# Fourteen of 24 groups of modulation vectors: from TensorE in four stages to VectorE inside the first MLP

## What is computed

```python
silu_c, silu_cc = silu(c), silu(c_ctx)                   # two vectors of 1024
for i in range(2):
    mod_x = silu_c @ w_mod[i] + b_mod[i]                  # 6 x 1024 values
    mod_c = silu_cc @ w_mod[i] + b_mod[i]
    # shift, scale, gate of the mixer; shift, scale, gate of the MLP
    hx = rmsnorm(x) * (1 + sc_x) + sh_x                   # the same for ctx
    yx = conv_module(hx) if i == 0 else attention(hx, hc)
    x = x + g_x * rmsnorm(yx)                             # ctx too in layer 0
    fx = rmsnorm(x) * (1 + scf_x) + shf_x
    x = x + gf_x * rmsnorm((silu(fx @ w1) * (fx @ w3)) @ w2)
```

## Time and profile before

| | |
|---|---|
| median of 3 runs | 1949.99 us (1949.28 to 1951.88) |
| the profiled execution's own time | 1947.4 us |
| its span in the profile | 1945.6 us |
| mean granted TensorE clock | 0.993 |
| busy, share of the span | PE 97%, PEld 86%, DVE 62%, ACT 49%, POOL 27% |

### The profile page before, as it was taken

How to read it: one execution, slowest core, us unless ns; L and a number is a source line. 1 busy time by engine, 2 the same in 40 slices (tenths; PEclk the granted TensorE clock), 3 DMA queues, 4 the chain that set the end, 5 groups by cost and what they waited for, 6 DMA issues and landing times.

```text
span 1945.6 us, 35849 instructions
## 1 busy us (share of the span) xinstructions
PE 1881.6 (97%) x14632; PEld 1668.0 (86%) x14632; DVE 1203.7 (62%) x2360; ACT 957.1 (49%) x1713; POOL 519.0 (27%) x663
## 2 busy tenths in 40 slices
PE   6999999999999999999999999999999999999998
PEld 3866778888886957999988999999999899989997
DVE  4998753233338776745578655684748775667473
ACT  4414532232224476544456574564655566456464
POOL 1200100000001443100012223737372332364736
PEclk9999999999999999999999999999999999999999
DMA  9344442322234255655545445455554443545551
GB/s 355 127 151 177 151 162 98 98 92 94 96 98 173 88 217 187 225 184 185 177 159 175 141 134 170 163 172 181 188 165 162 175 143 128 174 141 184 188 178 58
DMA packets 84545, 307.24 MB, mean 158 GB/s; under 512 B 9376, under 2 KB 10656, under 8 KB 84128
## 3 DMA queue, kind: packets, MB, share of 16 engines
q1 hardware_dynamic: 84384, 304.98, 46.6%
HBM read 303.89 MB, written 1.05 MB: 157 GB/s over the span
## 4 chain that ended last, share of the span: by engine, by line
PE 88%; DVE 5%; ACT 3%; DMA 2%; issue 1%; SPq 0%; DVEq 0%; ACTq 0%
PE pb L546 19%; PE pb L547 19%; PE pb L548 19%; PE pb L519 7%; PE pb L525 7%; PE pb L520 7%; PE pb L763 2%; DMA raw<-wstream 2%; PE pb L598 1%; DVE wlo L1932 1%; ACT whi L1267 1%; PE pb L925 1%; PE pb L1138 1%; PE pb L572 1%; PE pb L1151 1%
## 5 line engine op out<-in xcount | busy, mean ns | idle before, releaser
L546 PE MATMUL pb<-Hh,whi 128*128 128x256 f32 (+1 forms) x2288 | 695.6, 304 | 1.6 <-DVE SM L2536 1.4
L548 PE MATMUL pb<-Hh,wlo 128*128 128x256 f32 (+1 forms) x2288 | 688.6, 301 | 0.0
L547 PE MATMUL pb<-Hl,whi 128*128 128x256 f32 (+1 forms) x2288 | 688.6, 301 | 0.0
L1267 ACT ACTIVATE whi<-raw 128x1024 fp32r<-128x1024 f32 x468 | 489.5, 1054 | 316.9 <-PE pb L548 176.9
L1932 DVE TENSOR_TENSOR wlo<-raw,whi 128x1024 fp32r<-128x1024 f32 x330 | 428.0, 1302 | 334.3 <-ACT whi L1267 333.9
L2909 POOL TENSOR_TENSOR wlo<-raw,whi 128x256 fp32r<-128x256 f32 x552 | 413.8, 786 | 694.1 <-ACT whi L1267 693.2
L546 PEld LDWEIGHTS pb<-Hh,whi 128*128 128x128 f32 x2288 | 437.7, 191 | 22.8 <-issue 3.3
L547 PEld LDWEIGHTS pb<-Hl,whi 128*128 128x128 f32 x2288 | 437.8, 191 | 14.9
L548 PEld LDWEIGHTS pb<-Hh,wlo 128*128 128x128 f32 x2288 | 437.8, 191 | 15.0
L2933 POOL TENSOR_TENSOR X<-X,tmpb 128x512 f32<-128x512 f32 (+1 forms) x21 | 23.9, 1139 | 580.8 <-DVE tmpb L2098 580.7
L519 PE MATMUL pb<-Hh,whi 128*128 128x256 f32 (+1 forms) x544 | 165.8, 326 | 3.9 <-ACT Hh L1335 2.6
(11 more groups left out here) (338 smaller groups left out, 2940.1 us busy)
## 6 DMA issues: line engine op xcount, KB each, us to landing
raw<-wstream SPq DMA_DIRECT2D x572, 512.0 KB, 3.6
X<-xin SPq DMA_DIRECT2D x2, 1024.0 KB, 8.8
out<-X SPq DMA_DIRECT2D x8, 128.0 KB, 1.8
CON<-consts SPq DMA_DIRECT2D x1, 926.0 KB, 8.1
VEC<-vecs SPq DMA_DIRECT2D x1, 694.0 KB, 9.0
CON<-consts SPq DMA_DIRECT2D x1, 147.0 KB, 3.6
VEC<-vecs SPq DMA_DIRECT2D x1, 88.0 KB, 1.9
```

The costliest lines, as they stand in the source:

```text
L546: e.matmul(dst, hi, xh, start=k == 0, stop=False)
L547: e.matmul(dst, hi, xl, start=False, stop=False)
L548: i = e.matmul(dst, lo, xh, start=False, stop=k == kt - 1)
L1267: e.activation(whi[:, s % NPIECE, :], raw[:, p % NRAW, :], ACT.Copy).then_inc(sig("act_hi", ("hi", p)), 1)
```

## The change

F is now groups 10 and 11, A is 12 to 15, T is 16 to 23. VectorE computes them in the first MLP: it multiplies each 128x512 block of weights in `raw` by the silu of c (for F and A also of c_ctx), one scalar per partition, and adds the product to an accumulator in SBUF, eight blocks on one another (`mod_rows`). F's four accumulators lie in Y, which isn't used until the first `down` tiles; A and T have four and three buffers of `tmpb`, used in two and three turns. The sum over the 128 partitions is then made by TensorE (`vsum`): one matmul per accumulator, with a stationary operand of 32 columns of which one is ones (`pick`), into a strip of a bank. ScalarE's copy and the turn (`vturn`) follow as before. The weights' pieces ("vraw") are strewn over the stream of the MLP by `VAFTER`; VectorE does a piece's products just before the split of the piece that follows it (`lo_to`). No look-ahead ends at them (`on_pe`). All `feed`, `bite` and `mod_tr` of F, A, T0, T1 and G go. The matmuls of S0, S1, C and N stay. The first number of an entry of VMODS says how many vectors each block serves.

```diff
+MODS = {..., "F": (10, 2, 1), "A": (12, 4, 1), "T": (16, 8, 1)}
+VMODS = {"F": (2, [(0, 1)]), "A": (2, [(0, 1), (2, 3)]), "T": (1, [(0, 1, 2), (3, 4, 5), (6, 7)])}
+VAFTER = {1: "FTFT", 2: "FTT", 3: "FT", 4: "FTT", 5: "FTT", 6: "FTT", 7: "FT",
+          **{("down", m): "AT" for m in range(3, 8)}, 9: "ATT", 10: "ATT", 11: "AT", 12: "T", 13: "AT", 14: "A",
+          16: "ATTT", 17: "ATT", 18: "ATT", 19: "AT", 20: "A", 21: "A"}
...
     def ffn(up, down, l, parts, after=lambda at: None):
+            group(ups[:FIRST])
+            after(j0 + FIRST // 2 - 1)
+            for i, t in enumerate(ups[FIRST:], FIRST):
+                group([t])
+                if i % 2:
+                    after(j0 + i // 2)
...
+    def rows_after(at):
+        for name in VAFTER.get(at, ()):
+            g, k0 = next(rows[name])
+            b.extend(("vraw", "w_mod", (g // 12,), k * 128, g % 12 * 512, 512, 512) for k in (k0, k0 + 1))
...
+            def vsum(name, part):
+                parts = VMODS[name][1]
+                if not part:
+                    bank("pst" if name == "F" else "pt", ("mod", name), ("row", name))
+                b = slots.at(("mod", name))
+                w.wait_ge(*rest_in)
+                w.wait_ge(*on("vacc", name, part))
+                after = len(vmod_entries(name, part + 1)) if part + 1 < len(parts) else 0
+                for c, (m, s) in enumerate(vmod_entries(name, part)):
+                    i = e.matmul(b[32 * c:32 * c + 32, :], con("pick", 31 - 2 * m - s, 63 - 2 * m - s), vmod_acc(name, m, s),
+                                 start=not part, stop=c >= after)
...
-            feed("F")
-            sums3("y0", "r0", lambda: bite(1))
+            sums3("y0", "r0", lambda: None)
...
+            VSTEPS = {(0, 0, 15): lambda: vsum("T", 0), (0, 1, 7): lambda: vsum("A", 0), (0, 1, 11): lambda: vsum("T", 1),
+                      (0, 2, 11): lambda: vsum("T", 2), (0, 2, 12): lambda: vturn("T")}
...
+                    lin_first(downs[:FIRST], *dargs[:3], lambda k: [("hidh", l, j0 + k)], dargs[3], between=lambda k: (
+                        vsum(*("A", 1) if last else ("F", 0)) if l == 0 and (last or pi == 0) and k == 3 else None))
+                    if l == 0 and (last or pi == 0):
+                        vturn("A" if last else "F")
...
-            feed("A")
-            bite(1)
-            sums3("y1", "r1", lambda: bite(1))
+            sums3("y1", "r1", lambda: None)
             widen("y1", 512, ("rdone", "r1", 7))
-            bite(1)
-            mod_tr()
             widen("r1", 512, ("mt", "n2", 7))
...
-            feed("T0", "T1")
-            bite(2)
...
-                if P in (0, 1, 2, 4, 6, 8, 10, 12, 14, 17):
-                    bite(1)
-                if P in (10, 18):
-                    mod_tr()
...
+            def mod_rows(p):
+                for o, g, k in vrows[p]:
+                    name, m = vmod_of(g)
+                    segs, part = VMODS[name][0], vmod_part(name, m)
+                    for s in range(segs):
+                        if k == 0 and name != "F":
+                            buf(1.26, "ta" if name == "T" else "fa", ("va", name, m, s), ("vsum", name, part))
+                        t, src = vmod_acc(name, m, s), raw[:, p % NRAW, o:o + 512]
+                        by = csz[:, k, 2 * MOST - 2 + s:2 * MOST - 1 + s]
...
+                        w.wait_ge(*landed(p))
+                        if k:
+                            w.wait_ge(*on("vm", name, m, s, k - 1))
+                            i = e.scalar_tensor_tensor(out=t, in0=src, scalar=by, in1=t, op0=ALU.mult, op1=ALU.add)
+                        else:
+                            w.wait_ge(*on("sil"))
+                            i = e.tensor_scalar(t, src, by, None, ALU.mult)
...
             def lo_to(key, ahead=None):
                 for s in range(nxt[0], reach(key, ahead) + 1):
                     nxt[0] = s + 1
+                    while left and left[0] < split_of[s]:
+                        mod_rows(left.pop(0))
```

More of the change, by code:

```diff
@@ L69, in mod, with ffn @@
                 b.extend(("raw", "w_mod", (g // 12,), k * 128, g % 12 * 512, 512, 512) for k in range(8))
-    def ffn(up, down, l, parts, then=()):
+    rows = {name: iter([(g, k) for g in mod_groups(name) for k in range(0, 8, 2)]) for name in VMODS}
+    def ffn(up, down, l, parts, after=lambda at: None):
         j0 = 0
         for n in parts:
-            run([(name, (l,), c0 + j * 128) for j in range(j0, j0 + n) for name, c0 in up], FIRST, then=() if j0 else then)
-            run([(down, (l,), m * 128) for m in range(8)], FIRST, j0, n)
+            ups = [(name, (l,), c0 + j * 128) for j in range(j0, j0 + n) for name, c0 in up]
+            group(ups[:FIRST])
[4 more added lines that the diff above has]
+                    after(j0 + i // 2)
+            downs = [(down, (l,), m * 128) for m in range(8)]
+            group(downs[:FIRST], j0, n)
+            for m in range(FIRST, 8):
+                if j0 == 0:
+                    after(("down", m - 1))
+                group(downs[m:m + 1], j0, n)
+            if j0 == 0:
+                after(("down", 7))
             j0 += n
+    def rows_after(at):
+        for name in VAFTER.get(at, ()):
+            g, k0 = next(rows[name])
+            b.extend(("vraw", "w_mod", (g // 12,), k * 128, g % 12 * 512, 512, 512) for k in (k0, k0 + 1))
     w13 = (("ffn_w1", 0), ("ffn_w3", 0))
@@ L94, in stream_blocks @@
         group([t])
-    mod("T0", "T1")
     run([("attn_wo", (0,), m * 128) for m in range(8)], FIRST)
-    ffn(w13, "ffn_w2", 1, FFN1, ["G"])
+    ffn(w13, "ffn_w2", 1, FFN1)
+    assert all(next(r, None) is None for r in rows.values())
     for l in range(2):
@@ L360, in build, with vmod_of, vmod_entries, vmod_bands @@
             scratch(15 + 10 * l, acc=[5], ds=[6], sq=[0, 1, 2, 3, 4], t=[7, 8, 9, 10])
+        def vmod_of(g):
+            for name in VMODS:
+                if g in mod_groups(name):
+                    return name, g - MODS[name][0]
+        def vmod_entries(name, part):
+            segs, parts = VMODS[name]
+            return [(m, s) for m in parts[part] for s in range(segs)]
+        def vmod_bands(name):
+            return 32 * len(vmod_entries(name, 0))
+        def vmod_part(name, m):
+            return [i for i, ms in enumerate(VMODS[name][1]) if m in ms][0]
+        def vmod_acc(name, m, s):
+            if name == "F":
+                return Y[:, (2 * m + s) * 512:(2 * m + s + 1) * 512]
+            return slots.at(("va", name, m, s))
         def con(name, a=0, b=None, p0=0, p1=128):
@@ L612, in bite, with vturn @@
                 del pend[:n]
+            def vsum(name, part):
[9 more added lines that the diff above has]
+                                 start=not part, stop=c >= after)
+                points = [("modmm", name)] if part == len(parts) - 1 else []
+                i.then_inc(sig("pe_mod", ("vsum", name, part), *points), 1)
+            def vturn(name):
+                n, rows = MODS[name][1], vmod_bands(name)
+                t = slots.at(("row", name))
+                b = bank("pst", ("modtr", name), ("mods", name))
+                w.wait_ge(*on("row", name))
+                for j in range(4):
+                    i = e.matmul(b[:, 2 * n * j:2 * n * (j + 1)], t[0:rows, j * 128:(j + 1) * 128],
+                                 con("blocks", 0, 2 * n, 0, rows), start=True, stop=True)
+                i.then_inc(sig("pe_mod", ("modtr", name)), 1)
             def mod_tr(ring="pm"):
@@ L1456, in ffn @@
                             hi_to(("up", l, 1, 1), 4)
-                        if l == 0 and j == 0:
-                            row(1.25, "F")
+                        if (l, j) == (0, 21):
+                            row(1.25, "T")
                         t = buf(stage, "s", ("fs", l, j), ("hidl", l, j))
@@ L1472, in ffn @@
                         hi_to(("down", l, pi, m))
+                        if l == 0 and m == 0 and pi != 1:
+                            row(1.25, "A" if pi else "F")
                         if pi == 0:
+                            if l == 0:
+                                w.wait_ge(*on("vsum", "F", 0))
                             w.wait_ge(*on("lin", "down", l, pi, m))
@@ L1574, in scalar @@
                     turned(P)
-                if P in (8, 17):
-                    row(3, "T0" if P == 8 else "T1")
                 if P in (12, 14, 15, 16, 17):
@@ L2306, in ffn @@
                         lo_to(("down", l, pi, m))
+                        if l == 0 and (pi, m) in ((0, 4), (len(parts) - 1, 2)):
+                            mod_add("A" if pi else "F")
                         if pi:
```

67 lines of the change are left out of this document (37 added, 30 removed).

## The result

The changed kernel takes 1954.7 us as a median (17 runs), the kernel before 1950.8 on the same chip (17 runs). The ratio is 1.0024, 95% interval 1.0015 to 1.0034: slower by 3 to 7 us, about the size that can just be told from no change. The prediction was 1952.9. The profiled execution of the changed kernel took 1957.1 us, its span is 1955.2, against 1947.4 and 1945.6 before.

What follows compares the result with a forecast made beforehand. TensorE, busy 1881.6 of 1945.6 us, was taken as the bound. Terms -14.5 + 10.0 + 4.1 + 1.4 = +1.0, with clock losses of 1.7 and 0.2 +2.9, gave 1950.3 us profiled, 1952.9 as median; range 1943 to 1962.

Steps and rivals of the forecast that it cites:

- near balance: Whole kernel: every term stays within its bounds, 1947 to 1956 us; the forecast case, chance 0.48.
- First MLP: Removed halves 3.7 and F's turn 0.9 us; added sums and turns 10.0, start wait 4.1, its slow clock 1.4.
- Norm before it: Norm before the first MLP: sums no longer start behind a half, 0.8 us gained.
- Norm after it: Norm after the first MLP: root 1.8 us earlier and no turn of A to wait for; 2.7 gained, bounds 2.2 to 3.3.
- Attention's head: First scores sooner without two halves, less 0.8 us for VectorE's later last rope; 1.3 gained, 0 to 3.
- Loop and tail: Attention: loop's seven halves worth nothing, tail 2.1 us gained without T1's turn, one clock drop in the loop costing 1.7.
- Norm ahead of the second MLP and that MLP: Norm gains 0.9 us like the earlier one; the MLP gains 2.1 from one half and G's turn.
- the two rivals that I gave the smaller chances: Clock falls in the attention loop, 1956 to 1961 us, chance 0.18; VectorE bounds the MLP, 1960 to 1968, chance 0.09.
- the clock rival: Attention loop: idle 1.9 us drops the clock in three to five rounds, 1.7 each; 1956 to 1961 us, chance 0.18.
- signs of being wrong: Repeated waits for VectorE's splits in the MLP, slow clock in the attention, or an MLP lengthened by less than 6 us.
- The faster rival: Start wait of the MLP hardly there and the chains give more than followed; 1942 to 1946 us, chance 0.25.

Runs made afterwards that it cites:

- e2_late: Changed kernel with the first MLP's row pieces dealt out later, one F in place of F, T, F, T behind the first group; ratio 0.9994 to the kernel before.
- e11_bfill: Kernel before with more filler matmuls in the norm ahead of the second MLP, three before the second spread and four before the first matmul; ratio 1.0007.
- e1_cap: Changed kernel with the look-ahead of the weight splits stopped at wq's last piece, as in the kernel before; ratio 1.0018 to the kernel before.
- e6_head: Changed kernel with 14 filler matmuls in the attention's head, ahead of the third pair's scores; ratio 1.0014 to the kernel before.
- e7_clh: Changed kernel with the edits of e1_cap and e2_late and eight fillers at the attention's head; ratio 0.9978 to the kernel before.
- e12_tuned: e8_clhn with 3 fillers in the loop's five long rounds, 5 at the head, 4 in the first norm, 4 and 2 in the last; 1942.8 us, ratio 0.9962.
- e9_dprod: Changed kernel with 56 of T's products on VectorE issued twice; ratio 1.0038 to the kernel before.
- e8_clhn: e7_clh with five more fillers in the norm ahead of the first MLP, before the second spread; ratio 0.9976 to the kernel before.
- e13_less: e12_tuned with two fillers in each of the loop's five long rounds, four at the head, 3 and 3 in the norm ahead of the second MLP; ratio 0.9965.

## Why the prediction was right, and which steps were not

The median came 1.8 us above the forecast, within the case "near balance"; the ratio of 1.0024 is 4.7 us over the kernel before, where I had 2.9. That this is so near is in part luck. The steps that I forecast add up to +2.9, and in the two profiles the same stages add up to +6.6 (and the spans differ by 9.6): the first MLP and the norms are within 1.3 us each, but the attention came 5.2 us longer than I had it. Step by step, forecast against the stage table:

- **First MLP**, -3.7 - 0.9 + 10.0 + 4.1 + 1.4 = +10.9: measured +10.4. The sums cost 1.20 where I had 1.22, and the wait with its clock 5.84 against 5.5 (e2_late). The step held. Not in the sum were the first group's wait for ScalarE, which went from 1.28 to 0.41 (next step), and 0.5 without a known cause.
- **Norm before it**, -0.8: measured 0 up to the first matmul, and yet the step held. The second spread came 1.15 us sooner after pw2's last matmul (7.21 against 8.36), then half clock stretched the fillers ahead of the first matmul and held it back. But the kernel before waited at the next k-step:

```profile
238.88 0.50 PE L519 MATMUL pb<-Hh,whi 128*128 128x512 f32 x1 [1.28 <-ACT Hh L1335]
```

  From pw2's last matmul to there it was 16.11 us, in the changed kernel 15.34 (240.34): the 0.8 is there, booked in the MLP.
- **Norm after it**, -2.7: measured -4.0, outside my bounds of 2.2 to 3.3. The chain runs over VectorE. Its timelines, first of the kernel before (the rest stands in the earlier trace rows), then of the changed one:

```profile
616.73 0.87 DVE L2098 SCALAR_TENSOR_TENSOR tmpb<-Y,MA,pb 128x256 f32<-128x256 f32 x2 [0.22 <-PE pb L693]
```

```profile
626.91 0.77 DVE L2194 SCALAR_TENSOR_TENSOR tmpb<-Y,MA,pb 128x256 f32<-128x256 f32 x2
...
628.32 1.65 DVE L2194 SCALAR_TENSOR_TENSOR tmpb<-Y,MA,pb 128x256 f32<-128x256 f32 x4
629.89 0.74 DVE L2075 SCALAR_TENSOR_TENSOR MA<-MOD,VEC 128x8 f32<-128x8 f32 x2
630.67 1.66 DVE L2206 SCALAR_TENSOR_TENSOR tmpb<-X,MA,pb 128x256 f32<-128x256 f32 x4
```

  Counted from the MLP's last matmul (605.64 and 618.28), the third residual product ends 2.6 us sooner, where I had 1.8. The root gave 1.75 of them (it comes 0.94 after the squares, before 2.69); the squares themselves end 0.4 sooner, since two halves no longer stand ahead of the sums on which they follow; and VectorE no longer waits for the first spread, ahead of which TensorE had a half that waited 2.42 for its weights:

```profile
614.46 1.06 PE L598 MATMUL pb<-raw,csz 128*32 128x512 f32 x8 [2.42 <-DMA raw<-wstream]
615.46 1.16 PE L693 MATMUL pb<-tmpb,CON 128*128 128x128 f32 x8
```

  From that product's end to the next norm's first product it was 2.2 and is 0.7, 1.5 gained, the upper end of what I had allowed. How much of it all counts hangs on when the weights land: in e11_bfill's profile this norm of the kernel before took 19.51. Of VectorE's scaling I had said that 1.33 us stay; it took 0.74. This is no sign against the Trainium skill, SBUF — State Buffer, section "SBUF: two separate sides", with its exclusive lock: record by record, the longer of the two scalings starts at 629.89, lasts 0.67 and so ends with GpSimd's add (629.27 + 1.27), and before it started at 620.44, lasted 1.25 and ended with the second add (620.41 + 1.26). The lock costs what is left of the other's instruction, and that had moved.
- **Attention's head**, -1.3: measured +2.1. This is the step that failed. I had named the side effect of `stretch_end` and given VectorE's last rope 0.8 us of delay; the scale came 2.7 later (e1_cap), and the wait that was left without halves cost the clock 10.2 us at 1.2 GHz (e6_head, e7_clh), for which my sum had nothing. I had also tied the first scores to the scale. They don't need it: the changed kernel's start at 687.33, 0.5 after the last q sum and 4.6 ahead of the scale. The exponentials need it, and the third scores wait for those. With both mended the head is 1.7 shorter than before: the gain that I had counted was there, under two losses.
- **Loop and tail**, 0 - 2.1 and 1.7 for the clock: measured +1.4. Two falls of the clock stretched a round each by 1.6, where I had one. The last round went from 7.22 to 5.19, but behind a round that the clock had stretched; without a fall it is 5.69, and the whole stage 1.6 shorter than before (e12_tuned), where I had 2.1. The waits are 1.9 and the rounds 7.7, as forecast.
- **Norm ahead of the second MLP and that MLP**, -0.9 and -2.1: measured -2.2 with wo and -1.0. In e1_cap, where less of the slow stretch falls into the MLP, it is 1.96 shorter than before.

So the two rivals that I gave the smaller chances are settled otherwise than by the total: VectorE is no bound (e9_dprod), and the clock rival came true in part: slow clock in the attention stood among my signs of being wrong, and it showed, 10.2 us at the head and two falls in the loop where the rival had three to five. By the Trainium skill, TensorE: Matmul & The Clock Gate, section "A second HAM failure mode: psum-queue depth-cycling", short idle times between groups of matmuls make the clock swing. This case's runs agree in the loops that leave 1.9 us idle in a round, and show no fall in those that leave 0.9 or less. The faster rival's condition, no start wait, was not met; e2_late made it so and gave 0.9994, which on the prediction's 1949.99 is 1948.8 and still above that rival's 1942 to 1946.

What stays open is the start of the program: the last matmul of the convolution's stage ends between 221.5 and 226.2 us in profiles of kernels that are nearly the same up to there. Nine of the fourteen show 3.4 or 6.8 us at half clock near 25 us, but one without it (e8_clhn) took 224.6 as well, and no run looked for the cause.

## What to carry to other kernels

Work that an engine does while it waits is not free to remove: it may be what keeps the clock up, so cost the idle time that it leaves, and fill that with matmuls on a bank that nobody needs, counted to about the wait and no more. Then look one wait further on: fillers in the norm before the first MLP moved a matmul forward by 1.2 us and only lengthened the next wait. When something is taken out of a stream, look at what it had stopped: here a look-ahead ran on, and four splits landed in the one place where VectorE was late. And when work is dealt into a stream with room to spare on average, keep it away from the first tiles, where the engine that takes it has no head start.

## What the runs showed of the hardware that was not expected

- Where the clock falls is nearly the same from kernel to kernel, and hangs on single waits: 10.2 us at half clock behind the wait at the head in all six profiles of kernels that leave it unfilled, none in the five that fill it, 6.8 where 0.4 us of it stay (e13_less).
- A wait of 2.3 us at the head cost the same 10.2 us at 1.2 GHz as one of 5.0 (e1_cap against the changed kernel). The length of the wait is no measure of what the clock takes behind it.
- A slow stretch costs nothing where another engine sets the pace: in the norm after the first MLP the changed kernel shows 3.4 us and e1_cap 6.8 us at half clock, and the norm takes 14.41 in both. In the norm before it e2_late shows 3.4 us and e8_clhn none, and norm and MLP together take 387.5 in both.
